# A decoder block's first FFN: its down projection by seven block products, with the sums on GpSimd between the parameter tables

## The reference

```python
h = rms_norm(x, norm_ffn1_g)
gate, up = split(h @ w_ffn1_up)                     # 1024 x 5632
x = x + 0.5 * ((silu(gate) * up) @ w_ffn1_down)      # 2816 x 1024

h = rms_norm(x, norm_mix_g)
u, v, gates = split(h @ w_in)
y_a = GLU(gelu(s5_ssm(u, a, b, c, d, dt)) @ w_ssm_glu)   # diagonal state-space mixer
y_b = conformer_conv(v)                                  # gated, causal width 31, layer norm, pointwise
x = x + (sigmoid(g_a) * y_a + sigmoid(g_b) * y_b) @ w_out

x = x + 0.5 * swiglu_ffn(rms_norm(x, norm_ffn2_g), w_ffn2_up, w_ffn2_down)
out = rms_norm(x, norm_final_g)
```

## Time and profile before

| | |
|---|---|
| time, median of 3 runs | 2242.87 us (2239.89 to 2248.85) |
| the profiled execution | 2242.39 us, its span 2240.6 us |
| PE busy | 2192.9 us, 98% |
| DVE, ACT, POOL busy | 1620.6, 963.4, 620.6 us |
| first FFN's down part | 458.7 to 701.6 us of the span |

### The profile page before, as it was taken

One profiled execution on the slowest core, in us unless ns is written; L12 is line 12 of the kernel. 1 busy time (PEld: TensorE's weight loads), 2 busy tenths in 40 slices (PEclk: granted clock), 3 DMA queues, 4 the chain that ended last, 5 costly groups with the idle time before them and its releaser, 6 DMA issues.

```text
span 2240.6 us, 32120 instructions
## 1 busy us (share of the span) xinstructions
PE 2192.9 (98%) x10370; PEld 1811.8 (81%) x10370; DVE 1620.6 (72%) x2065; ACT 963.4 (43%) x1573; POOL 620.6 (28%) x720
## 2 busy tenths in 40 slices
PE   7999999999999999999999999999999999999998
PEld 6788888888888888888888788888878888887886
DVE  5867777755564999999998659454587787766667
ACT  5455555544554222222223224134355555544444
POOL 2888998700000000000000430000026663531000
PEclk9999999999999999999999999999999999999999
DMA  5223444367763345445435632553257765648654
GB/s 170 78 85 125 145 139 147 126 214 242 248 218 127 103 140 155 132 140 155 138 113 172 197 104 80 192 193 118 71 165 248 252 232 186 221 163 305 211 195 172
DMA packets 299581, 370.62 MB, mean 165 GB/s; under 512 B 26489, under 2 KB 198609, under 8 KB 299120
## 3 DMA queue, kind: packets, MB, share of 16 engines
q1 hardware_dynamic: 279280, 296.04, 41.6%
q0 software_dynamic: 19056, 69.42, 8.5%
q10 hardware_dynamic: 1168, 4.20, 0.5%
HBM read 259.73 MB, written 107.50 MB: 164 GB/s over the span
## 4 chain that ended last, share of the span: by engine, by line
PE 84%; DVE 8%; ACT 3%; DMA 3%; issue 2%; SPq 1%; DVEq 0%; ACTq 0%
PE PU L1347 10%; PE PU L1349 10%; PE PU L1348 10%; PE PU L1288 9%; PE PU L1290 8%; PE PU L1289 8%; PE PU L1227 3%; PE PU L1228 3%; PE PU L1229 3%; PE PD L1227 3%; PE PD L1229 3%; PE PD L1228 3%; PE PD L1423 1%; PE PD L1424 1%; PE PD L1425 1%
## 5 line engine op out<-in xcount | busy, mean ns | idle before, releaser
L1288 PE MATMUL PU<-Hhi,Whi 128*128 128x512 f32 x896 | 352.7, 394 | 2.6 <-DVE Hlo L2386 2.0
L1289 PE MATMUL PU<-Hlo,Whi 128*128 128x512 f32 x896 | 349.2, 390 | 0.0
L1290 PE MATMUL PU<-Hhi,Wlo 128*128 128x512 f32 x896 | 349.2, 390 | 0.0
L2365 DVE SCALAR_TENSOR_TENSOR XT<-XT,wq 128x1024 f32<-128x1024 f32 x240 | 313.2, 1305 | 8.2
L1288 PEld LDWEIGHTS PU<-Hhi,Whi 128*128 128x128 f32 x896 | 168.3, 188 | 40.8 <-issue 3.0
L1290 PEld LDWEIGHTS PU<-Hhi,Wlo 128*128 128x128 f32 x896 | 168.3, 188 | 35.0
L1289 PEld LDWEIGHTS PU<-Hlo,Whi 128*128 128x128 f32 x896 | 168.4, 188 | 34.8 <-issue 0.7
L1347 PE MATMUL PU<-Hhi,Dhi 128*128 128x512 f32 x480 | 187.2, 390 | 1.9 <-ACT s1b L1696 1.9
L1348 PE MATMUL PU<-Hlo,Dhi 128*128 128x512 f32 x480 | 187.0, 390 | 0.0
L1349 PE MATMUL PU<-Hhi,Dlo 128*128 128x512 f32 x480 | 186.9, 389 | 0.0
L1227 PE MATMUL PD<-Dhi,Ahi 128*128 128x512 f32 x352 | 138.4, 393 | 5.6 <-DVE Alo L2010 5.6
(11 more groups left out here) (416 smaller groups left out, 5218.2 us busy)
## 6 DMA issues: line engine op xcount, KB each, us to landing
d_act<-G SPq DMA_DIRECT2D x88, 256.0 KB, 2.1
XT<-in_w_ffn_down SPq DMA_DIRECT2D x88, 256.0 KB, 3.2
XT<-d_act SPq DMA_DIRECT2D x88, 256.0 KB, 3.4
Wraw<-in_w_ffn_up SPq DMA_DIRECT2D x80, 256.0 KB, 4.2
XT<-in_w_ffn_up SPq DMA_DIRECT2D x80, 256.0 KB, 4.4
Wraw<-in_w_in SPq DMA_DIRECT2D x32, 512.0 KB, 5.2
Wraw<-d_sb SPq DMA_DIRECT2D x55, 256.0 KB, 2.9
d_sb<-TAB POOLq DMA_DIRECT2D x21, 512.0 KB, 3.2
```

Of the source, the lines that this page charges most:

```text
L1288: mm(o_, Whi[s][:, side, k, :], Hhi[:, k, hs[h]], start=k == 0, stop=False)
L1289: mm(o_, Whi[s][:, side, k, :], Hlo[:, k, hs[h]], start=False, stop=False)
L1290: last = mm(o_, Wlo[s][:, side, k, :], Hhi[:, k, hs[h]], start=False, stop=k == KT - 1)
L2365: stt(CVb, z_, w_, CVb, ALU.mult, ALU.add).then_inc(m["conv"], 1)
```

## The change

The first FFN's down part is done by `down(FFN1)`, with seven products of 11 steps, in the order 3, 4, 5, 7, 1, 2, 6. GpSimd makes its 22 sets of sums, in a new order of its queue: 11 weight sets, tables 0 and 1, seven activation sets, table 2, two activation sets, table 3, the last two activation sets, tables 4 to 7. Between these groups it waits until the stores of the group before have landed. The ring's raw blocks of this part move to the buffers of the second pair of split weights (Whi1 and Wlo1), so the split of the mixer's second pair (`split_pair(R_MIX + 1, 1)`) moves behind the down part. All eight row blocks of the residual are in XT during the part, and are loaded by four quadrants of 1 MB (`rows_down`). The loads of the quadrants with `h` = 1 wait until ten activation sets are stored, since those sets use XT[:, 6:8]. The four quadrants (h, dh) are loaded in the order (0, 1), (1, 1), (0, 0), (1, 0), behind steps 4 and 7 of the first product and 2 and 5 of the second. `D_ROWS` gives this order.

```diff
-FFN1 = Proj(FT, 0, 0, 0, 0)
+FFN1 = Proj(FI, 0, 0, 0, 0)
-D_ORD = (3, 5, 7, 4, 1, 2, 6)
+D_ORD = {FFN1: (3, 4, 5, 7, 1, 2, 6), FFN2: (3, 5, 7, 4, 1, 2, 6)}
+D_ROWS_AT = {FFN1: ((0, 4), (0, 7), (1, 2), (1, 5)), FFN2: ((0, 4), (0, 7), (1, 4), (2, 4))}
+D_ROWS_BY = {FFN1: {1: 32, 2: 64}, FFN2: {1: 128, 2: 144, 4: 160}}
+A0 = {FFN1: 0, FFN2: FT}
+SUMS0 = {FFN1: 0, FFN2: 48 * FI}
...
+    WRd = over("Whi1", 0, "WRd", [P, RING, HW])
+    WRa = over("Wlo1", 0, "WRa", [P, RING, HW])
...
     def xo(S, h, j):
-        return XT[:, j if S is FFN1 else 4 * h + j, :]
+        return XT[:, 4 * h + j, :]
...
-        def load_product(p, t):
+        def load_product(S, p, t):
...
             if p == 0:
-                sp.wait_ge(sb_st, 48 * (t + 1))
-            sp.wait_ge(rd_lo, n - (RING - 1))
-            sp.dma_start(raw_d(FFN2, slot), weights).then_inc(rd_raw[slot], 16)
+                sp.wait_ge(sb_st, SUMS0[S] + 48 * (t + 1))
+            wait(sp, rd_lo, n - (RING - 1))
+            sp.dma_start(raw_d(S, place(S, slot)), weights).then_inc(rd_raw[slot], 16)
+            if x == 3:
+                sp.wait_ge(act_saved[0], 16 * (A0[S] + 2 * t + 1))
+            if x == 4:
+                sp.wait_ge(act_saved[1], 16 * (A0[S] + 2 * t + 2))
+            if x == 5:
+                sp.wait_ge(sa_st, SUMS0[S] + 48 * (t + 1))
...
+        def rows_down(S, h, dh):
+
+            if S is FFN2:
+                sp.wait_ge(x_st, 16 * 2 * J)
+            sp.wait_ge(u_prod, 7 * (UBASE[S] + NSP))
+            if h:
+                sp.wait_ge(sa_st, SUMS0[S] + 48 * (FI - 1))
+            src = {FFN1: x_rows, FFN2: d_x2}[S][4 * h:4 * h + 4, :, hs[dh]]
+            sp.dma_start(XT[:, 4 * h:4 * h + 4, hs[dh]], src.rearrange("j c d -> c j d")).then_inc(xr_ld, 16)
...
+            for p in range(7):
+                for t in range(FI):
+                    if p or t >= RING:
+                        load_product(S, p, t)
+                    if (p, t) in D_ROWS_AT[S]:
+                        rows_down(S, *D_ROWS[D_ROWS_AT[S].index((p, t))])
+                    if (p, t) in behind:
+                        behind[p, t]()
...
-        for p in range(4):
-            proj_phase(sp, FFN1, p, load_step if p else first_steps,
-                       [{20: lambda: load_rows(FFN1, 0, x_rows)}, {3: mix_first},
-                        {3: lambda: mix_pair(0, 1), 20: next_rows}, {}][p])
+        down(FFN1, {(2, 0): mix_first})
+        mix_pair(0, 1)
         store_rows(FFN1, 1, d_x)
...
-        for q in range(KT):
-            tile_table(q)
-        tables_saved(pool)
...
+        TAKES = {FFN1: [("w", c) for c in range(FI)] + [("a", c) for c in range(FI)],
...
+        takes(FFN1, range(0, FI))
+        stored(FFN1, FI)
+        for q in (0, 1):
+            tile_table(q)
+        tables_stored(2)
+        takes(FFN1, range(FI, FI + 7))
+        stored(FFN1, FI + 7)
+        tile_table(2)
+        tables_stored(3)
+        takes(FFN1, range(FI + 7, FI + 9))
+        stored(FFN1, FI + 9)
+        tile_table(3)
+        tables_stored(4)
+        takes(FFN1, range(FI + 9, 2 * FI))
+        stored(FFN1, 2 * FI)
+        for q in range(4, KT):
+            tile_table(q)
+        tables_saved(pool)
...
         fast_ffn(FFN1, 0, "nf1", params)
-        proj(FFN1, "nmx")
+        down(FFN1)
```

More of the change, by code:

```diff
@@ L407, in one @@
                 behind[t]()
[L409 to L417, removed]
+        for t in range(S.steps):
             one(t)
@@ new lines, in _, with stored, load_take @@
+        made = lambda S, k, kind: SUMS0[S] + 48 * sum(1 for t in TAKES[S][:k] if t[0] == kind)
+        def stored(S, k):
+            wait(pool, sb_st, made(S, k, "w"))
+            wait(pool, sa_st, made(S, k, "a"))
+        def load_take(S, k):
+            kind, c = TAKES[S][k]
+            stored(S, max(k - 1, 0))
+            if kind == "w":
+                src = {FFN1: w_ffn1_down, FFN2: w_ffn2_down}[S][0][2 * c * P:(2 * c + 2) * P].rearrange("(a p) n -> p a n", p=P)
+            else:
+                for h in range(2):
+                    pool.wait_ge(act_saved[h], 16 * (A0[S] + 2 * c + 2))
+                src = rows_p(d_act[2 * c:2 * c + 2])
+            pool.dma_start(set_of(k).rearrange("p (a n) -> p a n", a=2), src).then_inc(pool_ld[k % 2], 16)
+            loads[k % 2] += 1
+            due[S, k] = 16 * loads[k % 2]
@@ new lines, in takes, with tables_stored @@
+        def takes(S, ks):
+            last = 2 * FI - 1
+            early = [k for k in ks if k != last]
+            for k in early[:2]:
+                load_take(S, k)
+            for k in ks:
+                take(S, k)
+                if k + 2 in early:
+                    load_take(S, k + 2)
+                if k + 1 == last:
+                    load_take(S, last)
+        def tables_stored(count):
+            for saved in (ba_saved, ca_saved, rot_saved):
+                pool.wait_ge(saved, 16 * count)
@@ L1158, in _ @@
         pool.wait_ge(t_lo, 8)
-        for k in range(2):
-            load_take(k)
-        for k in range(len(TAKES)):
-            take(k)
+        takes(FFN2, range(2 * FI))
     @block.tensor
@@ L2338, in _ @@
         fast_ffn(FFN1, 0, 0, 0, "nf1")
-        proj(FFN1, "nmx")
-        added_all(FFN1, 3)
+        down(FFN1, {(3, 9): lambda: split_pair(R_MIX, 0), (5, 9): lambda: row_scale("nmx", 0),
+                    (6, 9): lambda: turned("nmx", 0, 0), (6, 10): lambda: turned("nmx", 0, 1)})
+        for j in range(4):
+            gather(FFN1, 6, j)
         row_scale("nmx", 1)
```

374 lines of the change are left out of this document (161 added, 213 removed).

## The result

The changed kernel takes 2384.26 us (median of 4 runs, 2382.43 to 2385.78) against 2242.55 before: a ratio of 1.0627, 95% interval 1.0604 to 1.0651. The profiled run took 2384.13 us, with a span of 2382.3 (before 2240.6, so +141.7).

A forecast was written before the change was run, and what follows sets the result against it. TensorE, busy 98% of the span, was taken to bound the kernel. Down part: 627 + 8 + 187.7 + 3.5 + 3 + 12 = 841.2 instead of 701.6, +139.6; with 1 + 1, +141.6 on 2242.39: 2384 us, range 2345 to 2425.

The forecast's parts named there:

- theory A: First FFN's down part: SyncE's residual row load waits for ten activation sets, and GpSimd's queue sets when these are stored.
- Removed, 29.9 us: First FFN's down part on TensorE: 924 matmuls instead of 1056, 132 x 0.2267 = 29.9 us less.
- GpSimd's queue, 627 us: GpSimd's sums and tables added up in order: tenth activation set stored at about 627 us, bounds 595 and 643.
- The eight steps before: Down part's first product: TensorE can do eight steps, from 458.7 to 480.5 us, and then has no data.
- Restart, 8 us: After the wait: row quadrant, step 8's blocks, copies and subtractions take 8 us; TensorE works from 635, after 155 idle.
- The rest: Down part after restart: 69 steps, 187.7 us, transposes 3.5, plus 3 for the clock and 12 for VectorE's slower subtractions.
- The end of the down part: First FFN's down part ends at 841.2 us instead of 701.6, +139.6.
- The edits charged with 1 + 1: 1 us for the mixer's second pair split later (0 to 3), 1 for GpSimd's additions in the up part (0 to 4).
- VectorE as the bound (2410): Down part after restart: VectorE and GpSimd alternate strictly, 3.4 us a step, 38 us lost instead of 12; chance 0.12.
- The faster case: Down part: ten sets stored by about 472 us, nothing stalls, 2214 us; from 502 on the change loses; chance 0.02.
- The wait at the third product: Rows do not wait; third product's step 9 does, 92 us instead of 155, 2321; chance 0.03 with anything overlooked.
- Foretold signs: TensorE hole 480 to 635 us, queue wait about 150, GpSimd busy to about 790, TensorE busy 51 less, clock dip.

## Why the prediction was right, step by step

It said 2384.0 us for 2384.26. The mechanism is the one it named, and the experiments with other buffers, another order and quicker sets each moved the end in theory A's direction, by 32, 82 and 32 us. That the sum comes within 0.3 us is luck: its terms were off by up to 5 us, with opposite signs.

- *Removed, 29.9 us.* The version without sums gains 25 us with everything else in place, 2.6 us short of the sum for it; TensorE's busy time fell by 21.4 us, not the 51 foretold, for two reasons that the step left out: the 0.39 us of a matmul is not its share (starts are 0.23 us apart), and busy time at the half clock is longer.
- *GpSimd's queue, 627 us.* SyncE went on at 631.45. The first additions came at 206.36 (203.6 foretold), the first table at 359.52 (359), activation sets from 428.38 (427). The first loads were 2.5 us late, and the weight sets made up for it, at 14.1 us from one to the next, where 14.3 was charged. The missing 4 us lie in the sets after 440: landing waits of 6.2 and 7.6 us as the products' loads came in, where 2.0 was charged.
- *The eight steps before.* Foretold until 480.5; they lasted until 491.2 because of waits of 1.7, 1.5 and 4.0 us and a lower clock. The stall hides that: the idle time is 152.0 us for the 154.5 foretold, though it ends 8 us later.
- *Restart, 8 us.* It was 11.7 (631.45 to 643.17). The blocks of step 8, issued behind the row load of 1 MB, took 8.2 us to land, where the earlier trace rows had 3.3 to 3.7.
- *The rest.* 201.3 us from 643.17 to the mixer's first matmul at 844.44. Against 187.7 + 3.5 that is 10.1 us lost, where I charged 3 for the clock and 12 for VectorE: 15. The runs divide it otherwise too: 5.8 us of missing work behind 665 us with GpSimd computing, the rest before it, at and behind the restart.
- *The end of the down part*: 841.2 foretold, 844.4 found: +4.4 from the queue, +3.7 from the restart, -4.9 from the rest. The edits charged with 1 + 1 cost nothing that shows, and behind the down part 1 us was gained. So the 3.2 us were cancelled in their turn.
- *Rivals.* VectorE as the bound (2410) is out for this kernel: after the restart no wait of TensorE's for a subtraction is over 2.55 us. The Trainium skill's rule of an exclusive lock between the two engines (SBUF — State Buffer, section SBUF: two separate sides) agrees in kind: subtractions of two SBUF operands grew from 0.69 to 1.03 and 1.26 us, operations with a PSUM operand stayed at 0.68. The strict alternation that I made of it does not: a table would have taken 45 us and took 33.2 to 36.1, and TensorE would have lost 38 us. With 138 us of tables beside the products the runs show 6, with 137 us 7 to 9, and in the version with tables until the products' end 24 are lost in all.
- *The faster case.* I gave 502 us as the break-even, and the version with quicker sets, at 498.70, is still 1.5% slower. The 502 holds only if nothing is lost behind the wait: with my own 15 us (3 and 12) and 2 for the edits it would have been 485. That version took 13.1 us to restart instead of 8 and lost 24 instead of 15, and it took 7.7 us more than the changed kernel from the mixer's first matmul to ScalarE's first `XT<-XT`.
- *The wait at the third product* (2321) was worked out too low: 2352 measured.
- *Foretold signs.* The hole, its place and length, the wait of SyncE (159.4 us for "about 150"), GpSimd busy to 787 (790) and the clock at the restart were all there; TensorE's busy time alone fell by less than half of what I said.

## What to carry to other kernels

Work given to an idle engine is not free when it stands in a queue in front of something that others need. Add up that engine's queue, in its order, up to each result that is waited for, with the landing of its stores and the slower pace beside busy neighbours. Then do the same for the last thing in the queue: taking away one wait brought out the next (third product, then tables), and here the whole queue, 200 to 787 us, is longer than what it had to hide beside: VectorE came to the tables at 696 us in the version without sums. When an experiment takes a cost away, look at the trace for what it put in its place before reading its time: the silent GpSimd with twelve bunched stores seemed to show that contention is free.

## What the runs showed of the hardware

- GpSimd is slower beside VectorE too: a table took 26.8 us while VectorE stood idle (526.74 to 553.55), 29.6 and 29.9 beside the up part, and 33.0 to 36.1 beside the products (changed kernel, and the version with late tables).
- The two subtractions of a step don't suffer alike beside tables: the activations' 1.26 us, the weights' 1.03. I have no run that says why.
- GpSimd's wait for the landing of a set's last store was 1.9 to 2.3 us while the other engines stood still, and up to 7.6 with the ring's loads beside it (changed kernel).
- After 152 us of idleness, with the granted clock at 0.50, the first matmul took 0.76 or 0.77 us, and the next ones started mostly 0.43 us apart: six intervals in the changed kernel (to 645.87 us), 13 in the version with spread stores (from 644.48 to 650.16). The rise of the clock is not the same in like situations: seven intervals more, each 0.20 us longer than at the full clock, make 1.4 us between two such versions.
